# A hybrid decoder step: each projection by one fp32 matmul instead of three fp32r products

## The reference

```python
def swiglu(x, w_gate, w_up, w_down):
    return (silu(x @ w_gate) * (x @ w_up)) @ w_down       # 1024 -> 2816 -> 1024

x = x + 0.5 * swiglu(rms_norm(x, ln_ffn1), ffn1_gate, ffn1_up, ffn1_down)
z = rms_norm(x, ln_mix) @ w_in                            # 1024 -> 2848 columns
...                                                       # chunk gMLP, RWKV-7 recurrence
x = x + concat([ya, yb]) @ w_out
mk = rms_norm(mem, mem_norm) @ xa_k; mv = rms_norm(mem, mem_norm) @ xa_v   # 256 memory tokens
q = rms_norm(x, ln_xattn) @ xa_q
...                                                       # softmax(q mk^T) mv, 4 heads
x = x + o @ xa_o
x = x + 0.5 * swiglu(rms_norm(x, ln_ffn2), ffn2_gate, ffn2_up, ffn2_down)
```

## Time and profile before

| what | value |
|---|---|
| median of 3 runs | 2959.73 us |
| span of the profiled execution | 2956.9 us |
| PE busy | 2724.3 us (92%) |
| DVE, POOL, ACT busy | 1186.9, 1230.9, 527.8 us |
| moved by DMA | 150.24 MB, 51 GB/s mean |

### The profile page before, as it was taken

One profiled execution on the slowest core, in us unless ns is written; L12 is line 12 of the kernel. 1 busy time (PEld: TensorE's weight loads), 2 busy tenths in 40 slices (PEclk: granted clock), 3 DMA queues, 4 the chain that ended last, 5 costly groups with the idle time before them and its releaser, 6 DMA issues.

```text
span 2956.9 us, 45589 instructions
## 1 busy us (share of the span) xinstructions
PE 2724.3 (92%) x17867; PEld 2604.0 (88%) x17867; DVE 1186.9 (40%) x2064; ACT 527.8 (18%) x1098; POOL 1230.9 (42%) x949
## 2 busy tenths in 40 slices
PE   5999999999999964988888798987999999999998
PEld 5999999999999962887876398986899999999997
DVE  6332233133614359556555553153353312331333
ACT  4110011011301012332324223012121100100112
POOL 4444444444544356423332446400444444444442
PEclk8999999999999986999998699998999999999999
DMA  3111111111321100000001214222211111111111
GB/s 108 46 46 47 47 48 47 46 46 41 109 61 44 41 31 0 1 1 1 1 1 68 97 47 121 92 86 86 91 45 46 46 48 48 47 46 46 46 38 73
DMA packets 220686, 150.24 MB, mean 51 GB/s; under 512 B 10831, under 2 KB 211113, under 8 KB 219946
## 3 DMA queue, kind: packets, MB, share of 16 engines
q1 hardware_dynamic: 217850, 135.11, 15.2%
q10 hardware_dynamic: 2256, 13.71, 1.2%
q0 software_dynamic: 480, 0.05, 0.0%
HBM read 134.80 MB, written 14.04 MB: 50 GB/s over the span
## 4 chain that ended last, share of the span: by engine, by line
PE 87%; DVE 7%; ACT 2%; issue 2%; DMA 0%; POOL 0%; SPq 0%; DVEq 0%; ACTq 0%; POOLq 0%
PE bank L372 24%; PE bank L374 23%; PE bank L373 23%; PE bank L1101 3%; PE bank L1107 2%; PE bank L1094 1%; PE bank L1539 1%; PE bank L1508 1%; PE bank L1572 1%; DVE TT L1014 1%; PE bank L1161 1%; PE bank L1132 1%; PE bank L1172 1%; DVE z L829 1%; PE bank L1173 0%
## 5 line engine op out<-in xcount | busy, mean ns | idle before, releaser
L345 POOL TENSOR_TENSOR w_hi<-raw,cst 128x512 fp32r<-128x512 f32 x366 | 464.2, 1268 | 1231.5 <-PE bank L374 1051.4
L372 PE MATMUL bank<-h_hi,w_lo 128*128 128x344 f32 x2856 | 915.4, 321 | 8.9 <-issue 7.5
L374 PE MATMUL bank<-h_hi,w_hi 128*128 128x344 f32 x2856 | 914.0, 320 | 0.0
L373 PE MATMUL bank<-h_lo,w_hi 128*128 128x344 f32 x2856 | 913.4, 320 | 0.0
L372 PEld LDWEIGHTS bank<-h_hi,w_lo 128*128 128x128 f32 x2856 | 536.0, 188 | 10.9 <-issue 9.2
L350 POOL TENSOR_TENSOR w_lo<-raw,w_hi 128x512 fp32r<-128x512 f32 (+1 forms) x398 | 514.1, 1292 | 64.7 <-ACT w_hi L342 35.0
L374 PEld LDWEIGHTS bank<-h_hi,w_hi 128*128 128x128 f32 x2856 | 536.7, 188 | 1.1
L373 PEld LDWEIGHTS bank<-h_lo,w_hi 128*128 128x128 f32 x2856 | 535.0, 187 | 1.4
L374 PE MATMUL bank<-hid_hi,w_hi 128*128 128x344 f32 x1056 | 337.8, 320 | 0.0
L372 PE MATMUL bank<-hid_hi,w_lo 128*128 128x344 f32 x1056 | 337.7, 320 | 0.0
L373 PE MATMUL bank<-hid_lo,w_hi 128*128 128x344 f32 x1056 | 337.6, 320 | 0.0
(11 more groups left out here) (312 smaller groups left out, 3459.4 us busy)
## 6 DMA issues: line engine op xcount, KB each, us to landing
raw<-in_ffn_gate SPq DMA_DIRECT2D x88, 256.0 KB, 2.9
raw<-in_ffn_up SPq DMA_DIRECT2D x88, 256.0 KB, 2.9
raw<-in_ffn_down SPq DMA_DIRECT2D x80, 256.0 KB, 2.7
raw<-in_w_in SPq DMA_DIRECT2D x44, 256.0 KB, 2.8
cache<-in_cache_mem_k SPq DMA_DIRECT2D x8, 1024.0 KB, 4.9
cache<-in_cache_mem_v SPq DMA_DIRECT2D x8, 1024.0 KB, 4.9
x_save<-x ACTq DMA_DIRECT2D x1, 4128.0 KB, 12.5
x<-x_save ACTq DMA_DIRECT2D x8, 516.0 KB, 6.8
```

The lines of the kernel that those rows point to most:

```text
L345: nc.gpsimd.tensor_tensor(w_hi[part], raw[part], cst[:, C_ONE:C_ONE + 1, 0:ph["width"]].to_broadcast([P, nk, ph["width"]]), ALU.mult)\
L372: nc.tensor.matmul(out, b, hi, start=first, stop=False)
L373: nc.tensor.matmul(out, a, lo, start=False, stop=False)
L374: m = nc.tensor.matmul(out, a, hi, start=False, stop=last)
```

## The change

Each product becomes one fp32 matmul on the unsplit operands. All splitting operations go: POOL has nothing left to do in the projections, DVE makes no low parts, and ACT writes the normed activations, the mixer's output, the memory tokens and the attention output once. DVE writes the feed-forward hidden directly. The buffers `raw`, `w_hi`, `w_lo` become one buffer `wt` of four slots. SP now loads a slot when PE has finished with it (`w_used` for the first piece of a unit, `mm` for the second) where it waited for the split before. PE waits for the load itself.

```diff
@@ load_weights
                 for (slot, turn), (k0, nk) in zip(turns, split_k(ph["kt"])):
-                    sp.wait_ge(split_done[slot], turn)
-                    sp.dma_start(raw[:, slot, 0:nk, 0:ph["width"]],
-                                 w[:, k0:k0 + nk, ds(col, ph["width"])]).then_inc(raw_in[slot], 16)
+                    if slot % 2 == 0:
+                        sp.wait_ge(w_used[st], turn)
+                    else:
+                        sp.wait_ge(mm[st], i * len(ph["toks"]) + ph["mm0"][st])
+                    sp.dma_start(wt[:, slot, 0:nk, 0:ph["width"]],
+                                 w[:, k0:k0 + nk, ds(col, ph["width"])]).then_inc(w_in_sem[slot], 16)
...
-        def split_weights(g, ph, high=True, low=True):
...
@@ multiply
                     for k in range(nk):
-                        a, b = w_hi[:, slot, k, 0:width], w_lo[:, slot, k, 0:width]
-                        hi, lo = ph["hi"][:, k0 + k, t0:t0 + tn], ph["lo"][:, k0 + k, t0:t0 + tn]
-                        first, last = k0 + k == 0, k0 + k == kt - 1
-                        nc.tensor.matmul(out, b, hi, start=first, stop=False)
-                        nc.tensor.matmul(out, a, lo, start=False, stop=False)
-                        m = nc.tensor.matmul(out, a, hi, start=False, stop=last)
+                        m = nc.tensor.matmul(out, wt[:, slot, k, 0:width], ph["act"][:, k0 + k, t0:t0 + tn],
+                                             start=k0 + k == 0, stop=k0 + k == kt - 1)
...
-                    pe.wait_ge(split_done[slot], turn + 1)
+                    pe.wait_ge(w_in_sem[slot], turn * 16 + 16)
...
@@ gu_vector (gate and up as before, then)
-                    nc.vector.tensor_tensor(tmp[:, t, :], tmp[:, t, :], gate_s[:, t, :], ALU.mult)\
-                        .then_inc(S("prod"), 1)
-
-                def low(t):
-                    dve.wait_ge(S("hid_hi"), done + t + 1)
-                    nc.vector.tensor_tensor(lo[:, ds(i, 1), tslice(t)], tmp[:, t:t + 1, :],
-                                            hi[:, ds(i, 1), tslice(t)].bitcast(F),
-                                            ALU.subtract).then_inc(S("hid_lo"), 1)
...
+                    nc.vector.tensor_tensor(out[:, ds(i, 1), tslice(t)], tmp[:, t:t + 1, :],
+                                            gate_s[:, t:t + 1, :], ALU.mult).then_inc(S("hid"), 1)
@@ split_vector becomes square_vector
-            dve.wait_ge(S("x_hi"), 24 * e + c + 1)
-            nc.vector.scalar_tensor_tensor(out=lo[:, k, tslice(t)], in0=x[:, k, tslice(t)],
-                                           scalar=v_col(gain, k), in1=hi[:, k, tslice(t)].bitcast(F),
-                                           op0=ALU.mult, op1=ALU.subtract).then_inc(S("x_lo"), 1)
...
-        def post_pool(g):
...
@@ mem_scalar_b
                 act.wait_ge(S("memT"), k // 2 + 1)
-                if k % 2:
-                    act.wait_ge(S("mem_lo"), k)
-                nc.scalar.activation(mem_hi[:, k, :], bank[k // 2][:, (k % 2) * 256:(k % 2) * 256 + 256],
-                                     ACT.Copy, scale=v_col("mem_norm", k)).then_inc(S("mem_hi"), 1)
-
-        def mem_vector_b(dve):
...
+                nc.scalar.activation(memT[:, k, :], bank[k // 2][:, (k % 2) * 256:(k % 2) * 256 + 256],
+                                     ACT.Copy, scale=v_col("mem_norm", k)).then_inc(S("mem_made"), 1)
@@ att_vector
-                    for g in (0, 1):
-                        dve.wait_ge(S("o_hi"), 2 * m + g + 1)
-                        nc.vector.tensor_tensor(o_lo[:, 4 * g:4 * g + 4, c],
-                                                bank[4 + g][:, :].rearrange("p (k t) -> p k t", k=4),
-                                                o_hi[:, 4 * g:4 * g + 4, c].bitcast(F), ALU.subtract)\
-                            .then_inc(S("o_lo"), 1)
```

More of the change, by code:

```diff
@@ L105, in program @@
         ident = cst[:, C_ID, :]
[L108 to L109 removed]
+        memT = at("memT", [P, KD, NMEM], arena_z + 8 * ROW)
         qT = at("qT", [P, KD, T], arena_z + 8 * ROW)
@@ L194, in program @@
         ya_in = at("ya_in", [P, 4, T], arena_h + 4 * ROW)
-        y_hi = at("y_hi", [P, KD, T], arena_z + 8 * ROW, R)
-        y_lo = at("y_lo", [P, KD, T], arena_z + 16 * ROW, R)
+        yT = at("yT", [P, KD, T], arena_z + 8 * ROW)
         st_T = at("st_T", [P, 3, 4, P], arena_w)
@@ L223, in S @@
             return sems[name]
-        raw_in = [S(f"raw_in{i}") for i in range(4)]
-        hi_done = [S(f"hi_done{i}") for i in range(4)]
-        split_done = [S(f"split_done{i}") for i in range(4)]
+        w_in_sem = [S(f"w_in{i}") for i in range(4)]
         w_used = [S(f"w_used{i}") for i in range(2)]
@@ L234, in program, with phase @@
         total = {"unit": 0, "mm": [0, 0], "f": 0}
-        def phase(name, units, kt, src, hi, lo, toks=TOK, width=P):
-            ph = dict(name=name, units=units, kt=kt, src=src, hi=hi, lo=lo, toks=toks, width=width,
+        def phase(name, units, kt, src, act, toks=TOK, width=P):
+            ph = dict(name=name, units=units, kt=kt, src=src, act=act, toks=toks, width=width,
                       u0=total["unit"], mm0=list(total["mm"]), f0=total["f"])
@@ L277, in program @@
         wo = kview(A["w_out"][0])
-        wout = phase("wout", 8, 8, lambda s, i: (wo, (2 * i + s) * P), y_hi, y_lo)
+        wout = phase("wout", 8, 8, lambda s, i: (wo, (2 * i + s) * P), yT)
         xk, xv, xq, xo = (kview(A[n][0]) for n in ("xa_k", "xa_v", "xa_q", "xa_o"))
         MTOK = [(0, NMEM)]
-        memk = phase("memk", 8, 8, lambda s, i: (xk, (2 * i + s) * P), mem_hi, mem_lo, toks=MTOK)
-        memv = phase("memv", 8, 8, lambda s, i: (xv, (2 * i + s) * P), mem_hi, mem_lo, toks=MTOK)
-        xaq = phase("xaq", 8, 8, lambda s, i: (xq, (2 * i + s) * P), h_hi, h_lo)
-        xao = phase("xao", 8, 8, lambda s, i: (xo, (2 * i + s) * P), o_hi, o_lo)
+        memk = phase("memk", 8, 8, lambda s, i: (xk, (2 * i + s) * P), memT, toks=MTOK)
+        memv = phase("memv", 8, 8, lambda s, i: (xv, (2 * i + s) * P), memT, toks=MTOK)
+        xaq = phase("xaq", 8, 8, lambda s, i: (xq, (2 * i + s) * P), h)
+        xao = phase("xao", 8, 8, lambda s, i: (xo, (2 * i + s) * P), oT)
         ffn2 = ffn(2)
@@ L425, in step @@
                         .then_inc(S("silu"), 1)
-                for t in range(3):
-                    act.wait_ge(S("prod"), i * 3 + 3 * ph["f0"] + t + 1)
-                    nc.scalar.activation(hi[:, ds(i, 1), tslice(t)],
-                                         tmp[:, t:t + 1, :], ACT.Copy).then_inc(S("hid_hi"), 1)
             pairs(act, ph, step)
@@ L1835, in _ @@
             sample_pool(g)
-            post_pool(g)
-            for ph in (wout, memk, memv, xaq, xao, *(p for ab in ffn2 for p in ab)):
-                split_weights(g, ph, high=ph not in (memk, memv))
         NVDMA = 16 * (len(VROWS) + 1)
@@ L1946, in _ @@
             mem_scalar_a(act)
-            residual_scalar(act, 2, "ln_xattn", wout, h_hi)
+            residual_scalar(act, 2, "ln_xattn", wout, h)
             mem_scalar_b(act)
             rms_scalar(act, 2)
-            for ph in (memk, memv):
-                split_weights(act, ph, low=False)
             nat_scalar(act)
```

196 lines of the change are left out of this document (60 added, 136 removed).

## The result

The changed kernel takes 3399.82 us (median of 4 runs, 3399.01 to 3400.04) where the kernel before, run beside it, takes 2958.66 us (4 runs, 2957.28 to 2959.74). The ratio is 1.1492, with a 95% interval from 1.1476 to 1.1508. The forecast was 3405 us. The span of the profiled execution is 3397.8 us, 440.9 above that of before.

What follows compares the result with a forecast made beforehand. PE was taken as the bound, going between projection matmuls for 70% of the time. 2956.9 + 460 + 9 - 24 = 3402 us, plus 2.8 for the runs' median, gave 3405 us; range 3382 to 3438.

Steps and rivals of the forecast that it cites:

- the price of one fp32 product: PE's projections: 0.578 us against 0.471 for 344 columns, 0.432 against 0.360 for 256; +460 and +9 us.
- rival 1: The joints give nothing back, so the time is 3429 us; chance 0.10.
- Start: Program start: with POOL idle and no low parts, PE starts its first product at 33.1 instead of 43.11 us; -10 us.
- Mixer to wout: After the mixer's last output PE no longer waits for its low part and the first slot's split; -3.5 us.
- wout to memory: Before the memory projections, ACT no longer takes turns with DVE's low parts and weights need no split; -6.2 us.
- Attention: Low parts of 1.20 us leave the chain in three of eight token blocks, -3.6, plus -0.5 towards xao.
- Loads: Weight loads now wait for PE to finish a slot, one turn later; leeway judged enough, cost nothing.
- Rival 3: Loads come late in the memory projections, +19 us, giving 3424 us; chance 0.04.
- rival 2: Fp32 matmuls with new weight blocks cost 0.05 us more per product in a dense stream, giving 3626 us; chance 0.04.
- rival 4: An fp32 product costs one record, not two, so the kernel gets faster, 2136 us; chance 0.02.
- The joints: The few places where PE waits for other engines; removing splitting there gives back 23.8 us together, bounds 0 and 32.

Runs made afterwards that it cites:

- e1: Kernel before with only the three matmuls per product replaced by one fp32 matmul on the high parts, all splitting kept; 3428.23 us.
- e2: Changed kernel plus eight POOL operations with two inputs at the start, results unused; 3404.73 us.
- e3: Changed kernel plus eight POOL operations with one tensor input at the start, results unused; 3398.61 us.
- e7: Changed kernel with DVE's low parts of the first normed activations put back, results unused, POOL idle; 3399.67 us.
- e8: Changed kernel with both DVE's low parts and POOL's eight two-input operations put back at the start; 3407.2 us.
- e5: Changed kernel with DVE's low parts of the memory tokens and ACT's and PE's waits on them put back, weights unsplit; 3404.45 us.
- e4: Changed kernel with DVE's low-part subtractions in the attention put back, PE and SP waiting for them; 3404.12 us.
- e10: Kernel before with attention low parts moved behind the next maxima and ACT's memory high parts not waiting for low parts; 2948.2 us.
- e6: Kernel before with bf16 in place of fp32r for all high and low parts, three matmuls per product kept; 2807.99 us.

## Why the prediction was right

The whole rested on the price of one fp32 product. It was read from the distances of an existing fp32 matmul of the same shape, and it held to 0.0004 us: 461.4 + 9.2 us measured, 460 + 9 forecast. e1 shows it alone: 3428.2 us, where rival 1 had put 3429 for a kernel with no joint improved.

**Start (-10, was -9.0).** PE's first product came at 34.08 us, not 33.1. The cause I named, slow DVE sums while POOL splits, is shown by e2 and e3, and its partner, the low parts, by e7 and e8. I had counted on POOL idle and the low parts gone together, without saying what each is worth. The result was 1 us off. The step is the length of the first group: 8.7 us was forecast (6.8 and 1.9), while ACT's second group starts 9.4 us after its first (15.91 and 25.30), since DVE's last sum ends 0.6 us behind ACT; I had put that in for the second group and not for the first. Another 0.3 us is that ACT's first gain came later in this execution, which no edit explains.

**Mixer to wout (-3.5, was -4.5).** 3.3 at the wait. The mixer itself was 1.2 us shorter, from the last `w_in` product to the last `yT` 612.0 us where it was 613.2, which I had not looked for.

**wout to memory (-6.2, was -6.5 and 2.5 more).** e5 shows the turns of ACT and DVE as 3.65 us of it. The 2.5 us is the clock, and the step that failed is that I counted a wait as only its own length: the windows show that PE went on at half clock behind it, and e5, which has the longer idle time back, has 2.3 us of it back.

**Attention (-4.1 with xao, was -6.9).** The same omission: my sum left this term at the time of the operations removed, and the traces have two groups 1.6 us shorter on top of it. e4 confirms the three low parts and shows a group at half clock again behind one of them, not behind both. Part of the size is luck, since the stage varies by 1.5 us between traces of the same code.

**Loads (0, was 0).** PE shows no wait for `wt` after the first unit. At the memory projections DMA moved 143 GB/s (150 forecast), the records came 0.216 us apart. Rival 3 fell. So did rival 2, with 0.289 us in all dense stages, and rival 4, since each fp32 product has two records. SP's waits at the weight loads (line 318) come to 2332 us, all ended by PE.

The joints together gave 28.7 us where 23.8 was forecast, 0.14% of the time, and the span of 3402 us came out at 3397.8. The median lies 2.0 us above that span where I had added 2.8, the other part of the 5 us between 3405 and 3399.8.

## What to carry to other kernels

Price a matmul from the distance between the starts of records of that type and shape, found anywhere in the trace, and count how many records one instruction makes; the mean record length misleads, and so does counting instructions: here one took the place of three and cost 23% more. Busy time that is taken from engines with room in a PE-bound kernel gives time back only at joints, and there it may pay more than the operation's own length, since behind a shorter idle time PE's granted clock was mostly higher here. What the joints give can in part be had by reordering alone, as e10 shows for two of them; and where three products stayed, the type of the parts was the larger lever here (150 against 10 us), if the reduced precision is acceptable.

## What the runs showed of the hardware that was not expected

- A DVE sum with two inputs takes 0.52 us alone, and 1.41 (e2) to 1.57 us while POOL runs operations with two inputs. While POOL runs operations with one input (e3) it takes 0.52. The Trainium skill, "GPSIMD Engine Reference", section "1. Specifications", has POOL's SBUF interfaces shared with VectorE, with contention where a DVE instruction has two SBUF inputs. With a POOL operation of two inputs the trace agrees (e2). With one of one input it does not: in e3 the same DVE sum, which has two SBUF inputs, ran at its full 0.52 us, so in this case the condition on DVE's side was not enough by itself.
- An fp32r record costs 0.157 us for 344 columns and 0.120 for 256, 0.013 us above the columns at 2.4 GHz in both; a bf16 record of 344 has 0.0024 us (e6), and an fp32 record, which takes twice its columns, 0.0025 (0.2892 us).
- Groups of 32 matmuls in the attention took 5.4 us at granted clock 0.68 and 3.8 us at 1.00. Both of the groups ahead of which the change cut PE's idle time from 2.35 to 1.15 us went from the one to the other. Over all traces six of eight groups behind 2.35 us were slow and none of 19 behind 1.15 us. At equal idle times both clocks occur: e4 has one of each at 2.35 us, and the changed kernel has 3.81 and 5.44 us behind 2.71 us (groups at 2277.96 and 2296.01 us). What decides between them is open.
